# Two-layer hybrid block on one core: the matmul operands' tiles placed at odd multiples of 64 bytes

## What is computed

```python
h = _rmsnorm(x, pre_norm_g)
proj = jnp.einsum('bsd,de->bse', h, w_in)
(q_a, c_kv, k_rope, z_mla, c_in, b_gate, c_gate, z_conv, g_mla, g_conv) = jnp.split(proj, cuts, axis=-1)
q = jnp.einsum('bsr,re->bse', _rmsnorm(q_a, q_a_norm_g), w_q_b)
kv = jnp.einsum('bsr,re->bse', _rmsnorm(c_kv, kv_a_norm_g), w_kv_b)
...
y_mla = jnp.einsum('bse,ed->bsd', attn * silu(z_mla), w_o_mla)
y_conv = jnp.einsum('bse,ed->bsd', b_gate * conv * silu(z_conv), w_o_conv)
merged = sigmoid(g_mla) * y_mla + sigmoid(g_conv) * y_conv
x = x + _rmsnorm(merged @ w_out, post_norm_g)
```

## Time and profile before

| | |
|---|---|
| median of 3 runs | 2014.66 us (2014.21 to 2016.21) |
| the profiled execution | 2014.4 us |
| its span, first to last instruction | 2013.1 us |
| mean granted TensorE clock | 0.995 |
| PE, PEld busy | 98%, 96% |
| DVE, ACT, POOL busy | 58%, 43%, 14% |
| HBM | 335.09 MB read, 6.29 MB written, 170 GB/s |

### The profile page before, as it was taken

One profiled execution on the slowest core, in us unless ns is written; L12 is line 12 of the kernel. 1 busy time (PEld: TensorE's weight loads), 2 busy tenths in 40 slices (PEclk: granted clock), 3 DMA queues, 4 the chain that ended last, 5 costly groups with the idle time before them and its releaser, 6 DMA issues.

```text
span 2013.1 us, 37092 instructions
## 1 busy us (share of the span) xinstructions
PE 1972.3 (98%) x15786; PEld 1936.3 (96%) x15786; DVE 1158.5 (58%) x1707; ACT 875.0 (43%) x1264; POOL 291.5 (14%) x320
## 2 busy tenths in 40 slices
PE   7999999999999999999999999999999999999999
PEld 6999999999999999999999989999999999999987
DVE  5765656555554445654554564576456676564644
ACT  5544454444444334444444443446443333444443
POOL 2110010202010002300112242030011132020200
PEclk9999999999999999999999999999999999999999
DMA  7465445455555555555565564443554443556564
GB/s 243 138 191 175 152 152 157 153 179 182 184 183 181 187 186 180 179 187 181 188 220 179 165 200 137 138 146 105 157 179 137 127 135 126 179 184 189 183 230 157
DMA packets 175647, 343.79 MB, mean 171 GB/s; under 512 B 10478, under 2 KB 19050, under 8 KB 174954
## 3 DMA queue, kind: packets, MB, share of 16 engines
q1 hardware_dynamic: 174106, 337.16, 53.0%
q10 hardware_dynamic: 1376, 4.26, 0.6%
HBM read 335.09 MB, written 6.29 MB: 170 GB/s over the span
## 4 chain that ended last, share of the span: by engine, by line
PE 84%; issue 5%; DVE 3%; ACT 2%; POOL 2%; POOLq 0%; ACTq 0%; DVEq 0%
PE bank L1256 83%; ACT w_hi L1581 1%; DVE w_lo L1884 1%; POOL arena L2479 1%; DVE arena L2155 1%; POOL scratch L2476 0%; POOL acc_b L2497 0%; POOL arena L2516 0%; POOL stats L2425 0%; DVE arena L2261 0%; DVE best L2259 0%; DVE scratch L1986 0%; ACT arena L1687 0%; PE bank L1463 0%; DVE arena L2204 0%
## 5 line engine op out<-in xcount | busy, mean ns | idle before, releaser
L1884 DVE TENSOR_TENSOR w_lo<-w_raw,w_hi 128x1024 fp32r<-128x1024 f32 (+2 forms) x644 | 784.6, 1222 | 794.2 <-ACT w_hi L1581 792.9
L1581 ACT ACTIVATE w_hi<-w_raw 128x1024 fp32r<-128x1024 f32 (+2 forms) x644 | 661.4, 1031 | 903.8 <-PE bank L1256 900.6
L1256 PE MATMUL bank<-hb_hi,w_hi 128*128 128x256 f32 x2448 | 701.1, 286 | 0.1
L1256 PE MATMUL bank<-hb_lo,w_hi 128*128 128x256 f32 x2448 | 694.8, 284 | 0.0
L1256 PE MATMUL bank<-hb_hi,w_lo 128*128 128x256 f32 x2448 | 694.8, 284 | 0.0
L1256 PE MATMUL bank<-ob_hi,w_hi 128*128 128x256 f32 (+1 forms) x2224 | 647.7, 291 | 7.0 <-DVE w_lo L1884 4.3
L1256 PE MATMUL bank<-ob_hi,w_lo 128*128 128x256 f32 (+1 forms) x2224 | 628.7, 283 | 0.0
L1256 PE MATMUL bank<-ob_lo,w_hi 128*128 128x256 f32 (+1 forms) x2224 | 627.6, 282 | 0.0
L1256 PEld LDWEIGHTS bank<-hb_hi,w_hi 128*128 128x128 f32 x2448 | 471.2, 192 | 2.4 <-DVE w_lo L1884 1.6
L1256 PEld LDWEIGHTS bank<-hb_lo,w_hi 128*128 128x128 f32 x2448 | 471.3, 193 | 0.4
L1256 PEld LDWEIGHTS bank<-hb_hi,w_lo 128*128 128x128 f32 x2448 | 471.2, 192 | 0.0
(11 more groups left out here) (242 smaller groups left out, 1206.6 us busy)
## 6 DMA issues: line engine op xcount, KB each, us to landing
w_raw<-in_w_in SPq DMA_DIRECT2D x436, 512.0 KB, 3.5
w_raw<-in_w_out SPq DMA_DIRECT2D x64, 512.0 KB, 4.1
w_raw<-in_w_o_conv SPq DMA_DIRECT2D x32, 512.0 KB, 3.6
w_raw<-in_w_o_mla SPq DMA_DIRECT2D x32, 512.0 KB, 3.7
w_raw<-in_w_branch SPq DMA_DIRECT2D x32, 512.0 KB, 3.5
w_raw<-in_w_kv_b SPq DMA_DIRECT2D x16, 512.0 KB, 3.7
w_raw<-in_w_q_b SPq DMA_DIRECT2D x16, 384.0 KB, 3.2
arena<-x_kept SPq DMA_DIRECT2D x2, 2048.0 KB, 9.7
```

The lines of the kernel that those rows point to most:

```text
L1256: return nc.tensor.matmul(dst, lhsT, rhs, start=start, stop=stop, skip_group_check=True)
L1581: act(dst, src, ACT.Copy).then_inc(S_("w_hi"), 1)
L1884: tt(low, src, high.bitcast(F32), ALU.subtract).then_inc(S_("w_lo"), 1)
```

## The change

Both activation buffers are placed anew. hb becomes one tensor with 16 unused columns (64 bytes) ahead of the tiles and 16 behind; its tile stride stays 1024 bytes. ob's tile stride becomes 288 columns, 1152 bytes, and all its 256-column operands now use columns 16 to 271; h2_all stays at columns 0 to 271. To make room kr1 moves into the arena, over a part that held x at the start, and its evacuation waits for the store of x and for the sum of squares. hb takes 128 bytes more, ob 2048 more, and 1024 are saved. No instruction is added, removed or moved.

```diff
+ODD = 16
...
-        self.hb_hi, self.hb_lo = sb("hb_hi", [P, KT, S], F32R), sb("hb_lo", [P, KT, S], F32R)
-        self.ob_hi, self.ob_lo = sb("ob_hi", [P, KT, T], F32R), sb("ob_lo", [P, KT, T], F32R)
+        hb = sb("hb", [P, ODD + 2 * KT * S + ODD], F32R)[:, ODD:ODD + 2 * KT * S].rearrange("p (k n) -> p k n", k=2 * KT)
+        self.hb_hi, self.hb_lo = hb[:, 0:KT, :], hb[:, KT:2 * KT, :]
+        self.ob_hi, self.ob_lo = (sb(n, [P, KT, T + ODD], F32R)[:, :, 0:T] for n in ("ob_hi", "ob_lo"))
...
-        self.kr1 = sb("kr1", [P, S])[:, :]
...
+        self.kr1 = r(68, 1, S)
...
-        return self.ob_hi[:, k, 0:S], self.ob_lo[:, k, 0:S]
+        return self.ob_hi[:, k, NMETA:T], self.ob_lo[:, k, NMETA:T]
...
-        out_by(s, m.kr1, m.R, done["r1"])
+        out_by(s, m.kr1, m.R, done["r1"], done["x_kept"], done["x_sq"])
```

More of the change, by code:

```diff
@@ L1629, in latent_split @@
         sc.wait_ge(*done["cols"])
-        act(m.ob_hi[:, k, 0:S], m.LAT[:, k, :], ACT.Copy, scale=m.col(which + "a", t)).then_inc(S_("op_hi"), 1)
+        act(m.ob_hi[:, k, NMETA:T], m.LAT[:, k, :], ACT.Copy, scale=m.col(which + "a", t)).then_inc(S_("op_hi"), 1)
     def v(s):
@@ L1678, in conv_split @@
         sc.wait_ge(*done["lat_used"])
-        act(m.ob_hi[:, k, 0:S], m.u_t[:, t, :], ACT.Copy).then_inc(S_("op_hi"), 1)
+        act(m.ob_hi[:, k, NMETA:T], m.u_t[:, t, :], ACT.Copy).then_inc(S_("op_hi"), 1)
     def gate(s):
@@ L1999, in latent_split @@
         ve.wait_ge(*s["op_hi"])
-        stt(m.ob_lo[:, k, 0:S], m.LAT[:, k, :], m.col(which + "a", t), m.ob_hi[:, k, 0:S].bitcast(F32),
+        stt(m.ob_lo[:, k, NMETA:T], m.LAT[:, k, :], m.col(which + "a", t), m.ob_hi[:, k, NMETA:T].bitcast(F32),
             ALU.mult, ALU.subtract).then_inc(S_("op_lo"), 1)
     def kr(s):
-        out_by(s, m.kr1, m.R, done["r1"])
+        out_by(s, m.kr1, m.R, done["r1"], done["x_kept"], done["x_sq"])
     def q_nope(s):
@@ L2090, in conv_split @@
         ve.wait_ge(*s["op_hi"])
-        tt(m.ob_lo[:, k, 0:S], m.u_t[:, t, :], m.ob_hi[:, k, 0:S].bitcast(F32), ALU.subtract).then_inc(S_("op_lo"), 1)
+        tt(m.ob_lo[:, k, NMETA:T], m.u_t[:, t, :], m.ob_hi[:, k, NMETA:T].bitcast(F32), ALU.subtract).then_inc(S_("op_lo"), 1)
     def gate(s):
```

## The result

The changed kernel takes 1990.53 us (1990.04 to 1991.09, four runs) against 2014.90 us (2014.21 to 2016.21, four runs) before: a ratio of 0.9878 with an interval of 0.9861 to 0.9895, 24.4 us less. The profiled execution has a span of 1989.3 us where it was 2013.1, and a granted clock of 0.994 (0.995). From here on, a *distance* is the time from the start of one weight product to the start of the next, inside a stage and without waits; a *position* is that of a moving tile in bytes modulo 256, counted from the position of the stationary operand.

What follows compares the result with a forecast made beforehand. TensorE, busy 98% of the span, was taken to bound the kernel, with 11 to 13 ns per product beyond its columns. 25.7 + 9.4 - 1.3 = 33.8 us less than 2014.4 gave 1981 us, range 1942 to 2004.

Steps and rivals of the forecast that it cites:

- rival 1: All products: with no even tile between, the fast rate holds everywhere; about 74 us less, 1941 us; 20%.
- rival 2: All products moved to odd positions stay at the slow rate; about 10 us less, 2004 us; 16%.
- Rival 3: Position is not the cause, or acts only where it differs from the tile before; 2014 us; 7%.
- Rival 4: Faster TensorE idles more in the second half, granted clock falls to 1.2 GHz more often; slower, 24 falls 2021 us; 6%.
- Does the position of a tile matter?: Stage qi: position counts; even tiles cost 118.7 to 120.0 ns, odd ones about 113.3 or about 118, held through a unit.
- hb, 3.6 ns x 7152 = 25.7 us: hb's matmuls, first stage left out: from 120.0 to 116.4 ns, 25.7 us less; bounds 12.2 and 48.6.
- nothing but TensorE sets the pace: Stages of weight products only: other engines partly idle, w_lo waits 4.3 us in all; what a product gains, the program gains.
- Every entry seems to draw anew: hb's tiles at 64: each wait or side matmul draws one of two rates, so a mixture of 116.4 ns.
- ob, 1.8 ns x 5232 = 9.4 us: ob's 256-column matmuls, all odd afterwards: from 118.2 to 116.4 ns, 9.4 us less; bounds 0.5 more, 26.2 less.
- 272 columns, +1.3 us: ob's 1200 matmuls of 272 columns, all even afterwards: 1.1 ns added each, 1.3 us more; bounds 1.2 less, 3.7 more.
- Stationary operand, writers, kr1: 0: hb and ob as stationary operand: 0, at most 0.6 us; writers run in idle engine time; kr1's moved evacuation costs 0.
- The rule against it: Skill page: distance N / 2.4 plus about 2.5 ns, independent read ports; 109.2 ns wherever the tile lies, so gain 0.

Runs made afterwards that it cites:

- m1_offsets: Bare product stream writing zeros, no computation; moving tiles at eight positions, eight entries each: 120.0 ns at 0, 113.3 or 117.8 at 64 and 192.
- e2_ob_only: Against the kernel before, only ob moved (stride 1152 bytes, kr1 in the arena), hb as before: 2010.95 us, ratio 0.9979.
- m2_pairs: Bare product stream with other positions of hi tile, lo tile and weights: 64/64/64 at 120.0 ns, 0/0/64 at 113.3 or 117.8.
- m4_more: Bare product stream at 240 and at places around 112, plus 272 columns at eight positions: 117.2 to 130.0 ns (256 columns), 123.3 to 126.7 (272).
- e4_nudge: Changed kernel plus four one-column side matmuls, ahead of bgate2, zmla, wout and bb: 1998.06 us, ratio 0.9918 to the kernel before.
- e5_hb_112: Against the kernel before, only hb moved, by 112 bytes; ob and kr1 as before: 1974.61 us, ratio 0.9802.

## Why the prediction was right, and where its steps were off

The time was put at 1981 us, with 1942 to 2004 as the range, and is 1990.5. The sign and the mechanism hold; the sum was 33.8 us and 24.4 came. The terms of the table above differ from it by 6.6 (hb), 4.4 (ob), -1.0 (272 columns) and 0.2 us (wout2). The range is less safe than it says: by its own chances half of rivals 1 and 2 and all of 3 and 4 lie outside, which is 31 in 100 and not "about 2 in 10".

- **"Does the position of a tile matter?"** Yes, and now shown alone: m1_offsets has nothing else in it, and e2_ob_only puts hb back to 120.0. "Two rates, about 113.3 or about 118" is right to the digit: 113.3 and 117.8. What I called the position was the right thing only because w_hi and w_lo lie at 0; m2_pairs shows that it is the position against the weights.
- **hb, 3.6 ns x 7152 = 25.7 us.** The distance fell by 3.2 (119.9 to 116.7), which is 23.0 us. The other 3.9 are two things. 1.5 us lie in the first stage, which the step had left out: qa took 36.05 and now 37.50, and in the other kernels of the study 35.9 to 37.3 (37.22 with hb where it was before), so it reads as scatter of its waits for operands rather than as a price of the position. 2.4 were given back behind the faster products; the profile names 1.5 of them as idle time ahead of hb's products, for w_lo. I had read "nothing but TensorE sets the pace" from a wait of 4.3 us in the whole program; it is now 6.2.
- **"Every entry seems to draw anew"** is the sentence that failed, and that the mean it gave came near is in part luck: with hb alone, at the same position, hb's mean is 117.6 and not 116.7, which is 6 us more over the 7152 products. bb was to show units at 113 and others at 118, 44.7 us in all; it is one rate from end to end, 117.8, 45.23 us. oconv and gb were to take 89.4 and take 90.46 and 90.10. In the first layer the slow rate holds in every stage from bgate0 (216 us) to the wait in gmla (848 us), through side matmuls and through the change of buffer in oconv. The fast one begins behind that wait; it had also held in kva's first half, in cin0 and into cgate0. hb's mean of 116.7 is about one quarter of the products at 113.3 and three quarters at 117.8, in a few long pieces. Three tiles of one stage were too few to say how long a rate holds, and they came from a stream whose position changes with every unit, where, it seems, each change of position draws. That rival 2 (all slow) is the truth for most of hb and for bb, and rival 1 (all fast) for most of gmla, shows how wide the single draw is.
- **ob, 1.8 ns x 5232 = 9.4 us.** This is the term that was mis-sized: 5.0 us, a distance of 117.0 to 117.1 instead of 116.4. qi's rows came from units that stay on one tile; oconv and gb take 2 tiles in a unit, at 192 and 64 in turn. Unit by unit, such stages have two rates of their own, 117.8 (all of oconv) and 116.7 (omla from its second unit on; gb, from 117.8 to 116.7 in its fifth unit), and neither is 113.3. m2_pairs found the same for other mixtures: 117.1 to 118.9, with 120.0 for 0/64/0. The rates of one-position streams were carried over to streams of two positions.
- **272 columns, +1.3 us.** +0.3: 125.8 ns, not 127. m4_more has 125.1 to 125.3 at position 0 and 126.7 at 128, the two places that these tiles now have.
- **Stationary operand, writers, kr1: 0.** wout2 is 0.2 us longer. That the writers run in "the half" of the time in which their engines are idle holds for ScalarE; VectorE is busy for two thirds of bb in the earlier trace rows. Nothing came of it: VectorE's and ScalarE's busy times are 1156.5 and 874.3 us where they were 1158.5 and 875.0. The evacuation of kr waits for nothing new: in VectorE's timeline it follows its two clears at once, at 81.71 us, where it stood at 81.10 in the earlier trace rows.

```profile
81.15 0.27 DVE L2041 MEMSET arena<- 64x256 f32 x1
81.51 0.27 DVE L2042 MEMSET arena<- 64x256 f32 x1
81.71 0.35 DVE L1988 TENSOR_TENSOR arena<-bank,factor 128x256 f32<-128x256 f32 x1
```

- **Rival 3** (position is no cause) falls by m1_offsets. **Rival 4** (the clock) falls by the row at 1335: the mean granted clock is 0.994 where it was 0.995.
- **The rule against it.** In m1_offsets one instruction form at a clock of 1.00 takes 113.3 to 120.0 ns by position alone, in m4_more up to 130.0, and no stream of these runs came to 109.2, which is an estimate by the formula of the Trainium skill's page "TensorE: Matmul & The Clock Gate" (Back-to-back issue gap) for 256 columns. That section calls it the gap of an isolated matmul and says that in a stream the weight loads set the spacing too; these runs agree that a stream is not at the formula, and show besides that its spacing depends on the position, which the section does not speak of. That the position counts against that of the weights (m2_pairs) also speaks against the independence of the two reads that the same page of the Trainium skill states (Step-by-step: what each phase is for), as far as these products go.

Left open: why 112 is the one place tried that pulls a stream to 113.3; whether 144 alone makes the half of kv with stationary activations slower; what in a wait or a side matmul decides between the rates at 64 and 192; the other runs of e4_nudge. Not tried: h2, h2_all and the v half of kv at a better place than now: with a stride of 1280 bytes all their tiles would share a position (h2 at 112, h2_all at 48), for 6144 bytes more of each partition (whether they are free is open; the change had to move kr1 to find 2176); at the distances of e5_hb_112 the 3456 products of h2 would gain at most 3456 x (117.7 - 113.3) = 15 us, an estimate.

## What to carry to other kernels

Where TensorE runs back to back, choose the position of the moving tiles against that of the weights modulo 256 bytes, and keep it the same for all tiles and both halves: for float32r products of 256 columns the best place measured here is 112 bytes (113.3 ns a product in every bare stream, 113.3 to 114.4 in the stages that hold only such products; q and kv are slower), the same position as the weights costs 120.0. Measure with a bare stream over positions and over several ways of entering it before you size the gain: a place with two rates gives a time that depends on how each stage was entered, and may show as spread between runs. A rate taken from a stream that stays on one tile doesn't hold for one that alternates.

## What the runs showed of the hardware that I had not expected

- The rate is a state of the stream. At positions 64 and 192 the same products run at 113.3 or 117.8 ns for hundreds of microseconds, and in gmla the change from one to the other came at a wait of 0.24 us. With hb alone a wait of 0.25 us at the same point changed nothing.
- In the streams place 112 always ended at 113.3, and 108, 116 and 120 at 120.0 to 121.9; 104 had 130.0 after two of five entries.
- The distances repeat in short patterns: 114, 113, 113 at the fast rate and 118, 117, 118 or 119, 117 at the slow one.
- 113.3 ns may be a floor: no position, entry or kernel of this study had a steady distance below it for 256 columns, 6.7 ns above the 106.7 of the columns at this clock. For 272 columns the lowest was 123.3.
